# Norm, latents, values, keys and queries of the second token span moved from the front of the kernel into its own stage, and the query jobs made in pairs

## What is computed

```python
hp = rmsnorm(xp, norm_mix)
b_g, c_g, x_in, q_lat, kv_lat, kr_raw, gate_c, gate_a = split(hp @ w_in)
conv_y = short_conv(c_g * x_in, conv_w)               # 512 channels, width 3
ckv, kr = rmsnorm(kv_lat), rope(rmsnorm(kr_raw))      # 256 and 32 wide
cq = rmsnorm(q_lat)                                   # 384 wide
qn, qr = per_head_rmsnorm(cq @ w_uq), then rope of qr # 8 heads, 64 + 32
kn = per_head_rmsnorm(ckv @ w_uk)                     # 8 heads, 64
attn = softmax(qn.kn + qr.kr) @ (ckv @ w_uv)          # causal
x = x + (sigmoid(gate_c) * (b_g * conv_y) @ w_conv_out
         + sigmoid(gate_a) * attn @ w_attn_out) @ w_mix_out
# PEER: 8 heads, top 16 of 128 x 128 experts by product keys
x = x + sum(g * gelu(expert_u[e] . h) * expert_v[e])
```

## Time and profile before

| | us |
|---|---|
| three runs | 3588.64, 3578.63, 3588.51 |
| median | 3588.51 |
| the profiled execution, its own time | 3591.56 |
| its span, first to last instruction | 3589.8 |

### The profile page before, as it was taken

The page is one execution under the profiler, slowest core; times in us unless marked ns, Lnnn a source line. Parts: engine busy times, 40 slices in busy tenths (PEclk is TensorE's granted clock), DMA queues, the critical chain, the costliest instruction groups (busy, mean ns, idle before and its releaser), DMA issues.

```text
span 3589.8 us, 33854 instructions
## 1 busy us (share of the span) xinstructions
PE 3022.6 (84%) x9744; PEld 1699.4 (47%) x9744; DVE 2554.2 (71%) x5723; ACT 1369.0 (38%) x3998; POOL 1099.2 (31%) x1252
## 2 busy tenths in 40 slices
PE   8889886879999968668778898899688989778877
PEld 5378652445555534334444454445245545455421
DVE  2321489776777997567777777789987787756864
ACT  2230234872223334336665222334353444423343
POOL 0000133333332332133333243333343333333342
PEclk9889997889999988778899999999798898867999
DMA  3234599999999988779999999989999999989998
GB/s 133 67 100 141 189 421 399 395 395 386 422 422 393 365 326 321 264 287 400 400 410 421 404 412 422 422 370 421 377 413 408 388 411 400 383 344 422 422 422 364
DMA packets 240417, 1280.11 MB, mean 357 GB/s; under 512 B 46095, under 2 KB 69231, under 8 KB 104935
## 3 DMA queue, kind: packets, MB, share of 16 engines
q0 software_dynamic: 152064, 1107.36, 75.7%
q1 hardware_dynamic: 86438, 166.19, 13.1%
q10 hardware_dynamic: 1728, 4.39, 0.3%
HBM read 1264.44 MB, written 13.40 MB: 356 GB/s over the span
## 4 chain that ended last, share of the span: by engine, by line
PE 35%; DVE 25%; DMA 22%; ACT 6%; issue 5%; POOL 1%; SPq 0%; DVEq 0%; POOLq 0%; ACTq 0%
DMA tl_uv<-in_uv,tl_idx 21%; PE tl_f L1084 10%; DVE tl_uv L1861 10%; PE tl_f L1447 7%; DVE tl_acc L1842 4%; PE tl_f L1389 3%; PE tl_f L1475 2%; PE tl_f L1458 2%; PE tl_f L1145 2%; PE tl_f L1209 1%; PE tl_f L1258 1%; PE tl_f L1281 1%; DVE tl_eq L1961 1%; DVE tl_ti L1882 1%; DVE tl_ti L1893 1%
## 5 line engine op out<-in xcount | busy, mean ns | idle before, releaser
L1015 POOL DMA_INDIRECT tl_uv<-in_uv,tl_idx x1056 | 1051.8, 996 | 1922.7 <-PE tl_f L1084 1179.6
L1861 DVE CUSTOM_DVE_ANT_0 tl_uv<-tl_uv,tl_f 128x1024 f32<-128x1024 f32 x1056 | 1265.4, 1214 | 368.6 <-DMA tl_uv<-in_uv,tl_idx 354.1
L1084 PE MATMUL tl_f<-tl_uv,tl_diag 128*128 128x512 f32 (+1 forms) x2460 | 1275.4, 659 | 266.8 <-ACT tl_diag L1494 266.2
L1084 PEld LDWEIGHTS tl_f<-tl_uv,tl_diag 128*128 128x128 f32 (+1 forms) x2460 | 473.1, 203 | 902.6 <-issue 461.2
L1522 ACT ACTIVATE tl_ge<-tl_a 128x1 f32<-128x1 f32 x1056 | 210.1, 199 | 1221.8 <-DVE tl_a L1861 1219.4
L1842 DVE SCALAR_TENSOR_TENSOR tl_acc<-tl_uv,tl_w,tl_acc 128x1024 f32<-128x1024 f32 x433 | 554.7, 1281 | 94.9 <-ACT tl_w L1506 94.9
L1506 ACT ACTIVATE tl_w<-tl_ge,tl_weight 128x1 f32<-128x1 f32 x1024 | 301.6, 294 | 33.2
L1475 PE MATMUL tl_f<-H,w_tail 128*128 128x384 f32 (+2 forms) x1024 | 262.8, 411 | 9.9 <-DVE H L2270 9.7
L1494 ACT ACTIVATE tl_diag<-K,tl_w 128x128 f32<-128x128 f32 (+1 forms) x615 | 244.4, 397 | 59.4 <-PE tl_f L1084 39.7
L1447 PE MATMUL tl_f<-H,w_tail 128*128 128x256 f32 (+2 forms) x768 | 234.0, 461 | 1.0 <-DVE tl_ya L2132 1.0
L1475 PEld LDWEIGHTS tl_f<-H,w_tail 128*128 128x128 f32 x1024 | 179.2, 194 | 105.3 <-issue 39.2
(11 more groups left out here) (281 smaller groups left out, 2950.2 us busy)
## 6 DMA issues: line engine op xcount, KB each, us to landing
w_tail<-in_w_merge SPq DMA_DIRECT2D x80, 512.0 KB, 7.8
w_tail<-in_w_peer SPq DMA_DIRECT2D x64, 576.0 KB, 7.9
w_tail<-in_w_conv SPq DMA_DIRECT2D x36, 512.0 KB, 7.8
tl_uv<-in_uv,tl_idx POOLq DMA_INDIRECT x1056, 14.7
w_tail<-in_w_mix SPq DMA_DIRECT2D x32, 512.0 KB, 7.8
X<-in_cache SPq DMA_DIRECT2D x48, 128.0 KB
o_y<-tl_acc ACTq DMA_DIRECT2D x8, 512.0 KB, 7.7
w_lat<-in_w_lat SPq DMA_DIRECT2D x6, 512.0 KB, 3.4
```

Of the source, the lines that this page charges most:

```text
L1015: pool.indirect_dma_start(UV[:, u % RING, :], None, d["uv"], bass.IndirectOffsetOnAxis(ap=which, axis=0)).then_inc(landed[u % RING], 16)
L1084: mm = pe.matmul(Y[0:m, half * 512:(half + 1) * 512], DG[:, (pe_count[u] - 1) % DIAGS, 0:m], UV[:, u % RING, D + half * 512:D + (half + 1) ...
L1861: dve.tensor_tensor_reduce(UV[:, u % RING, 0:D], UV[:, u % RING, 0:D], HP[:], 1.0, 0.0, ALU.mult, ALU.add, A[:, t % 2, i:i + 1]).then_inc( ...
```

## The change

The second span joins `LAZY`: its norm, latents, values, keys and queries leave the front, which is then one chunk of 272 tokens, and stand at the head of stage 1. For both lazy spans the 20 jobs become 10 pairs. A pair fills one PSUM bank, is copied and squared by one instruction each, and is spread back and scaled in one bank. Tables (`JOB_AT`, `BACK_AT`) say at which of 20 steps each is made, and ACT and DVE take these steps with a lag of one unit (`LAG_JOB`) in place of 3. The eight squares of the norm have a buffer each. ACT's first job waits for one small store (`r_kept`), and for the stores of the values only at the second pass. `absorb` moves behind the first channel group of stage 2. `EDGE` and the count of units stay.

```diff
-LAZY = (2,)
+LAZY = (1, 2)
 FRONT = META + SPANS[LAZY[0]][0]
-CHUNKS = [(0, FRONT // 2), (FRONT // 2, FRONT // 2)]
+CHUNKS = [(0, FRONT)]
...
-        j_sq, j_root, j_swap = part(7 * WMAX, 2, HALF), part(8 * WMAX, 2, HALF)[0:16], SH[:, 9 * WMAX:9 * WMAX + HALF]
...
+        j_sq, j_swap, j_raw = part(7 * WMAX, 2, HALF), part(8 * WMAX, 2, HALF), part(9 * WMAX, NJ, HALF)
+        n_sq = part(0, KD, WMAX)
...
-        n_sq, n_root = gates_flat[:, 0:2 * WMAX].rearrange("p (k n) -> p k n", n=WMAX), gates_flat[:, 2 * WMAX:3 * WMAX]
+        n_root = gates_flat[:, 0:WMAX]
...
+        j_root = gates_flat[0:16, NJ * P:NJ * P + HALF]
...
+        PAIRS = [(p, j) for p in range(4) for j in (range(0, 4, 2) if p % 2 == 0 else range(4, NJ, 2))]
+        NPAIRS = len(PAIRS)
+        PASS_FIRST = [0, 2, 5, 7, NPAIRS]
+        JOB_AT = (0, 1, 2, 3, 4, 8, 9, 12, 13, 14)
+        BACK_AT = (4, 5, 7, 8, 9, 12, 13, 17, 18, 19)
+        JSTEPS = BACK_AT[-1] + 1
+        on = lambda table, t: [i for i, at in enumerate(table) if at == t]
+        closes = lambda i: i + 1 in PASS_FIRST
+        open_sums = lambda i: sum(1 for m in range(i + 1) if not closes(m))
         open_squares = lambda b: sum(1 for m in range(b + 1) if m not in LAT_LAST)
...
-        LSTEPS = 1 + NLAT + 3 + NJOBS + 2
+        LSTEPS = 2 + NLAT + TMAX + JSTEPS
+        JSTEP = 2 + NLAT + TMAX
...
+                                + [x for t in range(JSTEPS) for x in [(c, JOB, i) for i in on(JOB_AT, t)]
+                                   + [(c, JSUM, PAIRS[i][0]) for i in on(JOB_AT, t - 1) if closes(i)]
+                                   + [(c, JSPR, i) for i in on(BACK_AT, t)]])
...
-                order += [(c, CHAN, g) for g in range(NCV)]
+                order += [x for g in range(NCV) for x in [(c, CHAN, g)] + [(c, ABSB, b) for b in range(2)] * (g == 0 and c == NCH - 2)]
...
-        LTICK = [12] + [10] * NLAT + [4] * TMAX + [3] * NJOBS + [6, 3]
+        LTICK = [12, 12] + [10] * NLAT + [4] * TMAX + [5] * (JSTEPS - 1) + [24]
...
-        LAG_ACT, LAG_DVE, LAG_POOL = 3, 6, 8
+        LAG_ACT, LAG_DVE, LAG_POOL, LAG_JOB = 3, 6, 8, 1
...
                 for g in range(WRING, weights.ASK + 1):
                     weight(g)
                 sp.wait_ge(l_step, 13 * li + 6)
-                sp.dma_start(d["o_kr"][:, col], l_kr[0:ROPE, 0:w]).then_inc(l_kept, 16)
+                sp.dma_start(d["o_kr"][:, col], l_kr[0:ROPE, 0:w]).then_inc(r_kept, 16)
+                if w > NMAX:
+                    sp.dma_start(d["s_kr"], l_kr[0:ROPE, NMAX:w]).then_inc(r_kept, 16)
                 sp.wait_ge(l_step, 13 * li + 9)
...
-                    if half == 0 and w > NMAX:
-                        weight(weights.ABSORB)
                 if w > NMAX:
                     sp.wait_ge(s_asked, 1)
                     sp.dma_start(d["s_qrs"], s_rope).then_inc(s_kept, 16)
-                    sp.wait_ge(dve_took, dve_count[c, ABSB, 1])
-                    sp.dma_start(d["s_qabs"], s_abs).then_inc(s_kept, 16)
-                    sp.wait_ge(s_kept, 64)
-                sp.wait_ge(l_kept, 32 * (li + 1))
+                    sp.wait_ge(s_kept, 32)
+                sp.wait_ge(r_kept, 16 * (li + 1) + 16 * (w > NMAX))
+                sp.wait_ge(l_kept, 16 * (li + 1))
...
+                    if g == WRING and c == NCH - 2:
+                        sp.wait_ge(dve_took, dve_count[c, ABSB, 1])
+                        sp.dma_start(d["s_qabs"], s_abs).then_inc(s_kept, 16)
...
-            def job_sum(c, n, m):
-                p, j = JOBS[n]
-                if n == PASS_FIRST[p]:
+            def job_pair(c, i, m):
+                p, j = PAIRS[i]
...
+                bank_free(c, JOB, i)
+                nk, x = (KT, l_ckv) if j < 4 else (QT, l_cq)
+                for e in range(2):
+                    f = weights.flat(weights.lazy(c, weights.KEY if j < 4 else weights.ASK + (j + e - 4) // 3))
+                    first = (j + e) * KT if j < 4 else (j + e - 4) % 3 * QT
+                    for k in range(nk):
+                        mm = pe.matmul(F[:, i % 2, e * m:(e + 1) * m], f[:, (first + k) * P:(first + k + 1) * P],
+                                       x[:, k, p // 2 * m:(p // 2 + 1) * m], start=(k == 0), stop=(k == nk - 1),
+                                       skip_group_check=True)
+                mm.then_inc(proj, 1)
...
+            def pair_sum(c, i, m):
+                p, j = PAIRS[i]
...
+                for e in range(2):
+                    first = C_SUM4 + 20 - (8 + 4 * e) if j == 8 else C_SUM2 + 22 - 2 * (j % 4 + e)
+                    mm = pe.matmul(F[0:16, 2, 0:m], K[:, first:first + 16], j_sq[:, e, 0:m],
+                                   start=(i == PASS_FIRST[p] and e == 0), stop=(closes(i) and e == 1))
+                mm.then_inc(proj if closes(i) else j_summed, 1)
...
+            def pair_back(c, i, m):
+                p, j = PAIRS[i]
+                if i == 0:
...
                     pe.wait_ge(j_inv, 4 * nth(c) + p + 1)
...
-                pe.matmul(F[:, 3, 0:m], j_spread[:, j, :], j_root[:, p % 2, 0:m], start=True, stop=True).then_inc(proj, 1)
+                bank_free(c, JSPR, i)
+                for e in range(2):
+                    mm = pe.matmul(F[:, 3, e * m:(e + 1) * m], j_spread[:, j + e, :], j_root[:, 0:m], start=True, stop=True,
+                                   skip_group_check=True)
+                mm.then_inc(proj, 1)
 
...
                 m, at = w // 2, -PRE[c]
-                units(due(c, at, 0))
+                units(due(c, at + 1, 0))
                 bank_free(c, NORM, 0)
                 for k in range(KD):
                     pe.wait_ge(n_squared, KD * li + k + 1)
-                    mm = pe.matmul(F[:, 3, 0:w], K[:, C_MEAN:C_MEAN + P], n_sq[:, k % 2, 0:w],
+                    mm = pe.matmul(F[:, 3, 0:w], K[:, C_MEAN:C_MEAN + P], n_sq[:, k, 0:w],
                                    start=(k == 0), stop=(k == KD - 1))
-                    mm.then_inc(n_summed if k < KD - 1 else proj, 1)
+                mm.then_inc(proj, 1)
                 for b in range(NLAT):
...
+                for t in range(JSTEPS):
+                    units(due(c, at + JSTEP + t, 0))
+                    for i in on(JOB_AT, t):
+                        job_pair(c, i, m)
+                    for i in on(JOB_AT, t - 1):
+                        pair_sum(c, i, m)
+                    for i in on(BACK_AT, t):
+                        pair_back(c, i, m)
...
+            def absorb(c):
+                arrived(weights.lazy(c, weights.ABSORB))
+                pe.wait_ge(s_asked, 1)
...
+                    if g == 0 and c == NCH - 2:
+                        absorb(c)
...
+                act.wait_ge(ranked, c)
                 for k in range(KD):
-                    if k >= 2:
-                        act.wait_ge(n_summed, (KD - 1) * li + k - 1)
-                    act.activation(n_sq[:, k % 2, 0:w], X[:, k, META + a:META + a + w], ACT.Square).then_inc(n_squared, 1)
+                    act.activation(n_sq[:, k, 0:w], X[:, k, META + a:META + a + w], ACT.Square).then_inc(n_squared, 1)
+                units(due(c, at + 1, LAG_ACT))
...
                     act.wait_ge(proj, ready[c, LAT, b])
-                    if b == 0:
-                        act.wait_ge(ranked, c)
...
+                    if p:
+                        act.wait_ge(proj, ready[c, JSPR, PASS_FIRST[p] - 1])
+                    act.activation(j_root[:, 0:m], F[0:16, 2, 0:m], ACT.Sqrt, bias=K[0:16, C_EPS:C_EPS + 1]
                                    ).then_inc(act_took, 1)
...
+                def job_taken(i):
...
+                    act.wait_ge(proj, ready[c, JOB, i])
+                    both = F[:, i % 2, 0:2 * m].rearrange("p (e n) -> p e n", n=m)
+                    if i == 0:
...
-                            act.wait_ge(v_kept[i], 32 * (2 - i) * (li + 1))
-                        if c == NCH - 2:
-                            act.wait_ge(s_kept, 32)
-                    if n == PASS_FIRST[2]:
+                        act.wait_ge(r_kept, 16 * (li + 1) + 16 * (w > NMAX))
+                    if i == PASS_FIRST[1]:
+                        for e in range(2):
+                            act.wait_ge(v_kept[e], 32 * (2 - e) * (li + 1))
+                    if i == PASS_FIRST[2]:
                         act.wait_ge(k_kept, 32 * li + 16)
-                    if n == PASS_FIRST[3]:
+                    if i == PASS_FIRST[3]:
                         act.wait_ge(q_kept, 64 * li + 32)
-                    if n >= 2:
-                        if closes(n - 2):
-                            act.wait_ge(proj, ready[c, JSUM, JOBS[n - 2][0]])
+                    act.activation(j_raw[:, j:j + 2, 0:m], both, ACT.Copy)
+                    if i:
...
-                    if n in PASS_FIRST[1:]:
-                        job_root(p - 1)
-                units(due(c, at + LSTEPS - 2, LAG_ACT))
-                job_root(3)
```

(45 more changed lines are left out.)

161 lines of the change are left out of this document (50 added, 111 removed).

## The result

The changed kernel takes 3659.8 us in the median of four runs (3654.95 to 3666.6), the kernel before 3586.5 in its four. The ratio is 1.0199, 95% interval 1.0183 to 1.0215. So the change makes the kernel slower by 2.0%, where I had forecast 0.4% faster. In one later kernel (the edge at 140) one of the four executions took 11342.73 us where the others took 3723.0 to 3732.0, and it is left out.

What follows compares the result with a forecast made beforehand. No single engine bounds the kernel; each stage has its own limit (DMA, TensorE, DVE or a chain). Front minus 87, stage 1 plus 98, stage 2 minus 26 sum to minus 15: median 3574 us, range 3555 to 3592.

Steps and rivals of the forecast that it cites:

- The front, minus 87: Front: 272 columns in one pass in place of 656 in two, 87 us shorter, bounds 80 to 93.
- Stage 1, plus 98: Stage 1: gains a lazy part of 157 us, less 33, 8, 2 and 16 in the parts behind.
- The dense parts, minus 59: Stage 1 behind the lazy part: attention minus 33, channels and merge minus 8, mix minus 2, ranking minus 16.
- The ranking: Stage 1: bound by DVE; 12 dots and about 2 sums less there, minus 16 us.
- channels and merge, 216: Stage 1: 60 units for 72, TensorE binds, minus 8 us, to 216 with TensorE full.
- The lazy part, 157: Head of stage 1: 140 us of TensorE work at an 89% busy share takes 157 us, bounds 140 to 194.
- Stage 2, minus 26: Stage 2: lazy part plus 9, attention minus 17, channels and merge minus 9, mix minus 2, ranking minus 7.
- The one that said slower: Rival: chain does not fit between units, stage 1's lazy part takes 194 us, plus 22, 3611 us; chance 0.25.
- The rival that TensorE has slack in channels and merge: Stage 1: channels and merge run at DMA's pace, 192 us, lazy part at 140; minus 56, 3533 us; chance 0.17.
- The third rival, stage 2 without gain: Stage 2's lazy part takes 266 us and gives back what attention wins; 3600 us; chance 0.13.
- The drain that the Trainium skill puts at each switch of tables: ACT's table loads: another 1380 ns each; by it ACT would lose 43 us and the sum be minus 4.

Runs made afterwards that it cites:

- the edge at 140: The kernel before with the first edge at 140 units in place of 56, nothing moved: 3728.9 us, 1.0403 of before.
- The edge kernels: The kernel before with the first edge at 98 or at 140 units in place of 56, nothing moved: 3650.2 and 3728.9 us.
- the best chain tried: Changed kernel with lag 3, values in H, weight ahead of stores: 3605.3 us, 1.0037; with ticks 3 and 12, only third span lazy: 3574.2 us, 0.9953.
- the one attempt: Changed kernel with lag 3, values in H, weight ahead of stores, plus job steps at 3 ticks and 60 on the last: 3623.4 us.

## Why the prediction was wrong

**The front, minus 87: right**, 87.7 measured, and by its terms (latents from 21.3 to 49.4 us, 28 where 26 was said, keys and queries 40.0 for 40).

**Stage 1, plus 98: wrong, plus 152, and this step decided.** Two terms of it failed, and a third that it had put at nothing.
- *The dense parts, minus 59*: minus 35. Attention was read as bound by DMA because its share was 0.99, so that 14 units less would give 33 us. It gave 18, and 15 with the wait for its loads. Two waits of DVE, from the table of waits of the kernel before (595 to 820) and of the changed one (693 to 901):

```profile
DVE tl_uv L1861 <- DMA tl_uv<-in_uv,tl_idx: 34.9, 31, 4.4
DVE tl_acc L1842 <- ACT tl_w L1506: 3.2, 4, 1.8
```

```profile
DVE tl_acc L1859 <- ACT tl_w L1521: 32.4, 14, 4.0
DVE tl_uv L1878 <- DMA tl_uv<-in_uv,tl_idx: 6.6, 8, 2.2
```

Of the 34.9 us of waiting for gathers 28 went, but 29 us of waiting for the weights that ACT makes came in their place. ACT was busy 163 of 208 us there and TensorE 168, so neither is full, and which chain sets the 208 us is not shown. The ranking, read as bound by DVE's 222 of 242 us, lost 8.5 us of DVE work where 16 were counted, and got 2 us shorter by the windows, 4 by the marks. The edge kernels show both with nothing moved. The forecast held for channels and merge, 216, exactly.
- *The lazy part, 157*: 186. TensorE's work was sized rightly: 139.0 us busy in the first two windows, for 140. The share was not: I took 89%, as in the rest of stage 1, and it was 75% (139 of 185 us). I took the pairs and the tight spacing to remove the waits; the lag of one unit put new ones in, and the stores of values, counted inside the 157, were not covered. With lag 3 the part takes 13 us less, and with the weight ahead of the stores another 10.5: 159.5 us without the wait behind it.
- *The wait for attention's first loads*, 3.4 us in the changed kernel and up to 16.4 in the others, had no term.

**Stage 2, minus 26: wrong, plus 11.** The lazy part took 23 us more and not 9, by the same circle (53.1 us of waiting for the diagonals): with lag 3 it took 5 more, 13 us of wait for loads included. The parts behind gave back 12 and not 35. Attention there stayed at DMA's pace with 141 dots beside it in both kernels, where the table of due units had made me count seven fewer.

**The rivals.** The one that said slower named the right mechanism (ACT and DVE held behind the chain, lazy part up to 194) and a time, 3611, that is 49 us short. It kept the minus 26 for stage 2, where 37 are missing, and the minus 59, where 24 are; its lazy part of stage 1 was 8 too long. The stores that it named were half of it: in that part TensorE waited 28.6 us for the diagonals and 13.6 for ACT's squares, which stood behind the store of a tile of values. The rival that TensorE has slack in channels and merge is refuted: with 12 units less, DMA went from 1.01 to 0.95 and the part still took TensorE's 214 us, while weight loads were busy 121.8 of 216. The Trainium skill, "Perfetto Trace Analysis", "Identifying the Most-Contended Engine", judges TensorE's headroom by the share of weight loads and by the use of its peak rate. The prediction took the first alone, 56%, and by it DMA would be the bound; in this stretch the busy share of the matmuls told the truth. The third rival, stage 2 without gain, was right in that attention there gave nothing back, though the lazy part took 240 us and not 266. Its sum was wrong as written: 40 us more in the lazy part less the 35 behind is plus 5, not 0, and makes the whole plus 16, 3605 us.

The drain that the Trainium skill puts at each switch of tables ("ScalarE: Activation LUTs", "What ACT_TABLE_LOAD costs") does not show after the change either: where nothing else is waited for, the next ACTIVATE starts 0.01 to 0.02 us behind the load's end.

Left open: which chain sets the length of stage 1's attention, as no engine is full in it, and whether the move could pay with other spacing. Taking away the 16 us for which attention waits for its first loads is not enough: the one attempt gave back 4 of them. With the best chain tried, the move still cost 1.0037 against 0.9953 of before (with other ticks), and 36 us with equal ones.
